# Two pairs of feed-forward units per layer computed with seven block products instead of eight

## The chip, the cores and the metric

The kernel runs on one core of a Trainium2 chip. The metric is the device time of one execution in microseconds (us), from which a median over runs is taken. TensorE does the matrix products, VectorE (DVE) and ScalarE (ACT) the element-wise work, GpSimd (POOL) a few tiny operations, and SyncE's queue (SP) issues the transfers of the weights.

## The reference, cut to what matters

Four layers, each with a feed-forward block, an attention and a second feed-forward block; 256 tokens, width 1024, feed-forward width 2816, all in fp32:

```python
def swiglu(x, w_gate, w_up, w_down):
    return (jax.nn.silu(x @ w_gate) * (x @ w_up)) @ w_down
...
x = x + 0.5 * swiglu(rms_norm(x, norm_g[i, 0]), ffn_w_gate[i, 0], ffn_w_up[i, 0], ffn_w_down[i, 0])
...
x = x + mix @ w_o[i]
x = x + 0.5 * swiglu(rms_norm(x, norm_g[i, 2]), ffn_w_gate[i, 1], ffn_w_up[i, 1], ffn_w_down[i, 1])
```

So there are eight feed-forward blocks. The change touches their gate and up products.

## The kernel before

**Chunks.** All weights are one stream of chunks of 128 x 2048 fp32 (1 MB). Every fp32 product is made of three products of reduced-precision parts: high x high, high x low, low x high. A chunk is loaded by SP into one of three places of `raw`, ScalarE copies it rounded into `w_hi` (`hi`, L376), and VectorE subtracts that from the raw chunk into `w_lo` (`lo`, L629). `w_hi` and `w_lo` are rings of six chunks. SP loads chunk c into a place once the `lo` of chunk c - 3 is done. ScalarE may write a ring slot when TensorE has finished with the chunk six before (`slot_free`).

**Units.** A feed-forward block is cut into eleven units of 256 hidden columns. A unit has three chunks: gate, up (called "top" and "bottom") and down. Units 0 and 1 ("turned") are computed with the tokens on the partitions. Units 2 to 10 ("own") have the hidden columns on the partitions: `own_gate_up` (L1200 to L1205) runs, for each of two banks, eight steps with one matmul of 512 columns (high weights against high and low tokens) and one of 256 (low weights against high tokens). The gate goes to PSUM banks 0 and 1, the up half to banks 2 and 3. Then the down product of the unit before follows: 24 matmuls of 512 columns into `acc` (L1071 to L1073).

**Around a unit.** When the gate half is done, ScalarE copies its second halves out of PSUM (`gate_rest`, L435), VectorE adds (L726), ScalarE applies silu (L438). When the up half is done: ScalarE copies (L440), VectorE adds (L729) and multiplies (L732), ScalarE makes the high part `m_hi` (L443), VectorE the low part `m_lo` (L735). TensorE may start the next unit's gate when L726 is done (`gate_ready`), its up half when L729 is done (`up_ready`), and its down product when L735 is done (`h_split`). In between each engine splits the chunks of the coming units, in an order written out by hand: VectorE's `split_to(c)` means "do all `lo` up to chunk c", ScalarE's the same for `hi`. Every engine works through its own list strictly in order, so what stands behind a waiting instruction waits too. Units 4 to 9 run in a hardware loop of three turns of two units. After the last down product the block's output is added to x and the next input is prepared.

## Time and profile before

| what | value |
|---|---|
| median of 3 runs | 1964.34 us (1964.17 to 1964.35) |
| the profiled execution's own time | 1965.22 us |
| its span in the trace | 1963.4 us |
| granted TensorE clock, mean | 0.996 |
| TensorE / VectorE / ScalarE busy | 99% / 62% / 48% |

The span runs from the first to the last instruction of the trace; the profiled execution took 1.8 us more than its span, and 0.9 us more than the median. "Busy" counts the time in which at least one instruction of the engine runs. A matmul's duration in the trace is longer than the distance to the next one, since they are pipelined: what a stretch costs is read from starts, not from durations.

### The profile page before, as it was taken

The numbers are of one execution on the slowest core, as the hardware profiler recorded it, in microseconds if no ns is written. First come the engines' busy times: TensorE is split into PE (matmuls) and PEld (weight loads), VectorE is DVE, ScalarE is ACT, GpSimd is POOL, SyncE is SP. The second block draws the span as 40 slices with busy tenths as digits, with TensorE's granted clock in tenths as the row PEclk, the third lists the DMA queues.
The fourth block names the chain that finished last, engine by engine and source line by source line (L and its number), as shares of the span: only waits on it lengthen the run. The fifth ranks groups of instructions, "written<-read, shape, count | busy, mean of one in ns | idle before, by whom it ended". The sixth has DMA issues, their size and how long they took to land.

```text
span 1963.4 us, 26311 instructions
## 1 busy us (share of the span) xinstructions
PE 1945.8 (99%) x10556; PEld 1681.9 (86%) x10556; DVE 1219.4 (62%) x1179; ACT 949.7 (48%) x1018; POOL 41.1 (2%) x34
## 2 busy tenths in 40 slices
PE   9999999999999999999999999999999999999998
PEld 7888998888888898888888889988888888988887
DVE  6555657655755678755575555775557556557554
ACT  5444545444544444644454443454445444545443
POOL 0000000000000000100000000000000000000000
PEclk9999999999999999999999999999999999999999
DMA  7654443555455453555445543445554554535541
GB/s 253 234 188 186 157 152 150 206 186 187 186 186 186 168 193 109 185 199 192 172 177 189 191 152 129 171 169 206 186 188 172 193 192 150 194 128 193 191 187 71
DMA packets 49872, 348.80 MB, mean 178 GB/s; under 512 B 6145, under 2 KB 6401, under 8 KB 7937
## 3 DMA queue, kind: packets, MB, share of 16 engines
q1 hardware_dynamic: 49360, 346.54, 47.9%
q8 instruction: 61, 1.00, 0.2%
q10 hardware_dynamic: 432, 1.11, 0.2%
q14 instruction: 19, 0.15, 0.0%
HBM read 346.58 MB, written 1.05 MB: 177 GB/s over the span
## 4 chain that ended last, share of the span: by engine, by line
PE 97%; DVE 2%; DMA 0%; ACT 0%; issue 0%; POOLq 0%; POOL 0%; DVEq 0%; ACTq 0%
PE work L1202 27%; PE work L1200 12%; PE acc L1071 9%; PE acc L1073 9%; PE acc L1072 9%; PE work L1071 7%; PE work L1073 7%; PE work L1072 7%; PE work L1205 2%; PE acc L1115 1%; PE work L1385 1%; DVE w_lo L629 1%; PE work L1372 1%; PE work L1262 0%; DMA x<-x_dram 0%; PE work L1386 0%
## 5 line engine op out<-in xcount | busy, mean ns | idle before, releaser
L629 DVE TENSOR_TENSOR w_lo<-raw,w_hi 128x2048 fp32r<-128x2048 f32 x327 | 746.7, 2288 | 123.7 <-ACT w_hi L376 121.2
L1202 PE MATMUL work<-xn,w_hi 128*128 128x512 f32 x2304 | 795.6, 393 | 0.0
L376 ACT ACTIVATE w_hi<-raw 128x2048 fp32r<-128x2048 f32 x327 | 620.9, 1908 | 16.0 <-DMA raw<-stream_dram 16.0
L1200 PE MATMUL work<-xn,w_lo 128*128 128x256 f32 x2016 | 567.4, 281 | 0.0
L1202 PEld LDWEIGHTS work<-xn,w_hi 128*128 128x128 f32 x2304 | 417.6, 188 | 75.6
L1200 PEld LDWEIGHTS work<-xn,w_lo 128*128 128x128 f32 x2016 | 379.7, 188 | 13.9
L1071 PE MATMUL acc<-w_hi,m_hi 128*128 128x512 f32 x824 | 325.1, 395 | 1.2 <-DVE m_lo L845 0.6
L1073 PE MATMUL acc<-w_hi,m_lo 128*128 128x512 f32 x824 | 321.2, 390 | 0.0
L1072 PE MATMUL acc<-w_lo,m_hi 128*128 128x512 f32 x824 | 320.8, 389 | 0.0
L435 ACT ACTIVATE scratch<-work 128x512 f32<-128x512 f32 x72 | 43.2, 600 | 431.9 <-PE work L1202 431.9
L726 DVE TENSOR_TENSOR scratch<-work,scratch 128x512 f32<-128x512 f32 x72 | 49.8, 692 | 276.3 <-ACT scratch L435 276.3
L1073 PEld LDWEIGHTS acc<-w_hi,m_lo 128*128 128x128 f32 x824 | 154.7, 188 | 32.6
L1071 PEld LDWEIGHTS acc<-w_hi,m_hi 128*128 128x128 f32 x824 | 154.9, 188 | 32.1 <-issue 4.3
L1072 PEld LDWEIGHTS acc<-w_lo,m_hi 128*128 128x128 f32 x824 | 154.9, 188 | 30.8
L1071 PE MATMUL work<-xg,w_hi 128*128 128x256 f32 x512 | 149.7, 292 | 1.2 <-DVE m_lo L827 1.0
L1071 PE MATMUL work<-w_hi,xg 128*128 128x512 f32 x368 | 147.8, 402 | 0.0
L1072 PE MATMUL work<-xg,w_hi 128*128 128x256 f32 x512 | 145.8, 285 | 0.0
L1073 PE MATMUL work<-xg,w_lo 128*128 128x256 f32 x512 | 145.7, 285 | 0.0
L1073 PE MATMUL work<-w_hi,xg 128*128 128x512 f32 x368 | 143.9, 391 | 0.0
L1072 PE MATMUL work<-w_lo,xg 128*128 128x512 f32 x368 | 143.5, 390 | 0.0
L440 ACT ACTIVATE scratch<-work 128x512 f32<-128x512 f32 x72 | 43.1, 598 | 193.2 <-PE work L1202 193.2
L729 DVE TENSOR_TENSOR scratch<-work,scratch 128x512 f32<-128x512 f32 x72 | 49.8, 692 | 110.7 <-ACT scratch L440 110.7
(177 smaller groups left out, 1721.9 us busy)
## 6 DMA issues: line engine op xcount, KB each, us to landing
raw<-stream_dram SPq DMA_DIRECT2D x327, 1024.0 KB, 4.8
x<-x_dram SPq DMA_DIRECT2D x2, 512.0 KB, 7.7
raw<-stream_dram ACTq DMA_DIRECT2D x2, 512.0 KB, 7.4
cst<-consts_dram SPq DMA_DIRECT2D x1, 832.0 KB, 6.8
out_dram<-x SPq DMA_DIRECT2D x3, 256.0 KB, 2.4
final_gain<-final_gain_dram SPq DMA_DIRECT2D x1, 512.0 KB, 7.5
out_dram<-wide SPq DMA_DIRECT2D x1, 256.0 KB, 2.9
cst<-consts_dram ACTq DMA_DIRECT2D x1, 64.0 KB, 1.9
```

What stands on the lines that cost most here:

```text
L376: nc.scalar.activation(w_hi[:, c % RING, :], raw[:, c % RAW, :], ACT.Copy).then_inc(hi_ready, 1)
L435: nc.scalar.activation(gate_rest, own_bank(0)[:, :, T:2 * T], ACT.Copy).then_inc(gate_rest_ready, 1)
L440: nc.scalar.activation(up_rest, own_bank(1)[:, :, T:2 * T], ACT.Copy).then_inc(up_rest_ready, 1)
L629: nc.vector.tensor_tensor(w_lo[:, c % RING, :], raw[:, c % RAW, :], w_hi[:, c % RING, :].bitcast(F32), ALU.subtract).then_inc(lo_ready, 1)
L726: nc.vector.tensor_tensor(gate_sb, own_bank(0)[:, :, 0:T], gate_rest, ALU.add).then_inc(gate_ready, 1)
L729: nc.vector.tensor_tensor(up_sb, own_bank(1)[:, :, 0:T], up_rest, ALU.add).then_inc(up_ready, 1)
L1071: nc.tensor.matmul(dst, a_hi, b_hi, start=start, stop=False, skip_group_check=skip)
L1072: nc.tensor.matmul(dst, a_hi, b_lo, start=False, stop=False, skip_group_check=skip)
L1073: return nc.tensor.matmul(dst, a_lo, b_hi, start=False, stop=stop, skip_group_check=skip)
L1200: nc.tensor.matmul(bank[:, 0:T], lo, xn_hi[:, k, :], start=False, stop=False, skip_group_check=True)
L1202: ins = nc.tensor.matmul(halves(bank), hi, xn[:, :, k, :], start=k == 0, stop=k == DT - 1, skip_group_check=True)
L1205: nc.tensor.matmul(bank[:, 0:T], lo, xn_hi[:, k, :], start=False, stop=False, skip_group_check=True)
```

## The change

In each feed-forward block the units 4 and 5, and the units 8 and 9, are computed together (`SEVEN = 4, 8`). The gate and up columns of two units are 1024 columns; tokens (2 blocks of 128), contraction (2 halves of 512) and columns (2 blocks of 512, one for each unit) form a 2 x 2 by 2 x 2 block product. Instead of eight block products it takes seven, with sums of blocks as operands (Winograd's form). Called by their chunks, in TensorE's order (`PARTS`): b11, t1, t2, b21, t3, t4, b22. Each (`quarter`) is 12 matmuls of 512 columns.

- Four of the seven weight operands are sums of loaded chunks: t1 = b12 - b11, t3 = b22 - b12, t2 = t3 + b11, t4 = b21 - t2. VectorE makes them (`form`) during the unit ahead of the pair (unit 3 or 7), each in a place of its own: t3 over b12, t2 over b11 (both in `raw`), t1 and then t4 in a new place. b22 has a new place too. All seven are then split as other chunks are, so that a pair has seven gate and up chunks to split where two units had four. b11's and b21's places in `raw` come free when t4 is formed.
- Four sums of token blocks (`token_sums`) are formed and split once per block, during unit 2.
- The products come with tokens on the partitions. ScalarE copies two of them out of PSUM (`part_copied`), VectorE makes five sums (`pair_sums_ready`), silu and product are applied in four parts of 256 columns, and TensorE transposes the hidden values of both units (four transposes each) inside the gate half of unit 6 or 10. That unit then carries two down products.
- All hardware loops are gone; the same instructions are written out, SP's too.

The diff, cut to its core (the names of other new functions are in the text above):

```diff
-OWN_UNITS = UNITS - TURNED
-LOOPED = 4
+SEVEN = 4, 8
+PLAIN = [s for s in range(UNITS) if s not in SEVEN and s - 1 not in SEVEN]
+OWN = PLAIN[TURNED:]
+HIDDEN = [s for s in range(UNITS) if s not in OWN]
 PAIRS = D // COLS
-FFN_CHUNKS = 3 * UNITS
+FFN_CHUNKS = 3 * UNITS + 3 * len(SEVEN)
...
+FORMS = "t1", "t3", "t2", "t4"
+PARTS = "b11", "t1", "t2", "b21", "t3", "t4", "b22"
+PAIR_ORDER = *PARTS[:5], "down", *PARTS[5:]
+def ffn_order():
+    order = []
+    for s in range(UNITS):
+        if s in SEVEN:
+            order += [(what, s - (what == "down")) for what in PAIR_ORDER]
+        elif s - 1 in SEVEN:
+            continue
+        elif s - 2 in SEVEN:
+            order += [("top", s), ("down", s - 2), ("bottom", s), ("down", s - 1)]
+        else:
+            order += [("top", s), ("bottom", s)] + [("down", s - 1)] * (s > 0)
+    return order + [("down", UNITS - 1)]
+FFN_ORDER = ffn_order()
...
+            p = no * len(SEVEN) + SEVEN.index(j) if what in PARTS else None
+            if what in ("t1", "t4"):
+                uses.append((what, no, j, SUMS, None))
+            elif what == "b22":
+                uses.append((what, no, j, EXTRA, p + 1))
+            elif what in ("t2", "t3"):
+                uses.append((what, no, j, *places["b11" if what == "t2" else "b12"]))
+            else:
+                uses.append((what, no, j, len(users) % RAW, len(users) // RAW + 1))
+            for load in ("b12",) if what == "t1" else () if what in FORMS or what == "b22" else (what,):
+                r = len(users)
+                places[load] = r % RAW, r // RAW + 1
+                loads.append((load, layer, n % 3, j, r % RAW, users[r - RAW] if r >= RAW else None))
+                users.append(("form", len(FORMS) * (p + 1)) if load in ("b11", "b21") else
+                             ("lo", c0 + order.index(("t3", j)) + 1) if load == "b12" else ("lo", w + 1))
+            if what == "t1":
+                earlier = SEVEN.index(j) - 1
+                loads.append(("b22", layer, n % 3, j, EXTRA,
+                              ("gu", (no * len(PLAIN) + TURNED) * TB) if earlier < 0 else
+                              ("lo", c0 + order.index(("b22", SEVEN[earlier])) + 1)))
...
+                if what in FORMS:
+                    act.wait_ge(form_ready, (no * len(SEVEN) + SEVEN.index(j)) * len(FORMS) + FORMS.index(what) + 1)
+                else:
+                    act.wait_ge(b22_loaded if place == EXTRA else raw_loaded[place], 16 * count)
+                slot_free(act, c)
+                nc.scalar.activation(w_hi[:, c % RING, :], raw_at(place), ACT.Copy).then_inc(hi_ready, 1)
...
+                    after, ahead = s - 2 in SEVEN, s + 1 in SEVEN
+                    if not after:
+                        split_to(g + 3)
+                    if s == TURNED:
+                        hidden_hi(s - 1, unit_bank(s - 1, 0))
+                    if ahead and not after:
+                        split_to(g + 5)
+                    act.wait_ge(top_used, plain + 1)
+                    nc.scalar.activation(gate_rest, own_bank(0)[:, :, T:2 * T], ACT.Copy).then_inc(gate_rest_ready, 1)
+                    split_to(g + (3 if after else 6 if ahead else 4))
+                    act.wait_ge(gate_ready, own_u + 1)
+                    nc.scalar.activation(gate_sb, gate_sb, ACT.Silu).then_inc(own_silu_ready, 1)
+                    if s == TURNED:
+                        token_sums_hi()
+                    if after:
+                        split_to(g + 6)
+                    act.wait_ge(gu_psum, plain * TB + 2)
+                    nc.scalar.activation(up_rest, own_bank(1)[:, :, T:2 * T], ACT.Copy).then_inc(up_rest_ready, 1)
+                    if not after:
+                        split_to(g + (7 if ahead else 5))
+                    act.wait_ge(own_h_ready, own_u + 1)
+                    nc.scalar.activation(m_hi[:, u % 2 * 2:u % 2 * 2 + 2, :], up_sb, ACT.Copy).then_inc(h_hi_ready, 1)
+                    if after:
+                        split_to(g + 7)
...
+                    split_to(q + 5)
+                    copied(1, 0, first_part)
+                    split_to(q + 6)
+                    copied(2, 3, second_part)
+                    split_to(q + 7)
+                    act.wait_ge(part_psum, len(PARTS) * p + 4)
+                    nc.scalar.activation(pair_h[:], work[:, 0, 0:COLS], ACT.Silu).then_inc(pair_silu_ready, 1)
+                    split_to(q + 8)
+                    pair_silu(2, second_sum)
+                    split_to(q + 10)
+                    pair_silu(3, first_part)
+                    pair_silu(4, first_sum)
+                    hidden_hi(s, work[:, 2, :])
+                    hidden_hi(s + 1, work[:, 3, :])
...
+                if what == "t1":
+                    if j == SEVEN[0]:
+                        dve.wait_ge(gu_psum, (no * len(PLAIN) + TURNED) * TB)
+                    dve.wait_ge(raw_loaded[place["t3"]], 16 * USES[q + PAIR_ORDER.index("t3")][4])
+                    ins = nc.vector.tensor_tensor(raw_at(SUMS), b12, b11, ALU.subtract)
+                elif what == "t3":
+                    dve.wait_ge(b22_loaded, 16 * (p + 1))
+                    ins = nc.vector.tensor_tensor(b12, b22, b12, ALU.subtract)
+                elif what == "t2":
+                    dve.wait_ge(form_ready, len(FORMS) * p + 2)
+                    ins = nc.vector.tensor_tensor(b11, b12, b11, ALU.add)
+                else:
+                    dve.wait_ge(form_ready, len(FORMS) * p + 3)
+                    ins = nc.vector.tensor_tensor(raw_at(SUMS), b21, b11, ALU.subtract)
...
+                    if ahead:
+                        form("t1", g + 3)
+                        form("t3", g + 3)
+                        split_to(g + 4)
+                        form("t2", g + 3)
+                        split_to(g + 5)
+                    dve.wait_ge(gate_rest_ready, own_u + 1)
                     nc.vector.tensor_tensor(gate_sb, own_bank(0)[:, :, 0:T], gate_rest, ALU.add).then_inc(gate_ready, 1)
-                    split_next(1)
-                    dve.wait_ge(up_rest_ready, own_u + 1 + turn * 2)
+                    split_to(g + (6 if after or ahead else 4))
+                    if ahead:
+                        form("t4", g + 3)
+                    dve.wait_ge(up_rest_ready, own_u + 1)
                     nc.vector.tensor_tensor(up_sb, own_bank(1)[:, :, 0:T], up_rest, ALU.add).then_inc(up_ready, 1)
-                    dve.wait_ge(own_silu_ready, own_u + 1 + turn * 2)
-                    dve.wait_ge(up_ready, own_u + 1 + turn * 2)
+                    dve.wait_ge(own_silu_ready, own_u + 1)
+                    dve.wait_ge(up_ready, own_u + 1)
                     nc.vector.tensor_tensor(up_sb, up_sb, gate_sb, ALU.mult).then_inc(own_h_ready, 1)
-                    split_next(2)
-                    dve.wait_ge(h_hi_ready, u + 1 + turn * 2)
+                    if not after and not ahead:
+                        split_to(g + 5)
+                    dve.wait_ge(h_hi_ready, u + 1)
                     nc.vector.tensor_tensor(m_lo[:, u % 2 * 2:u % 2 * 2 + 2, :], up_sb,
                                             m_hi[:, u % 2 * 2:u % 2 * 2 + 2, :].bitcast(F32),
                                             ALU.subtract).then_inc(h_split, 1)
-                for turns, body in ffn_steps(step, c0):
-                    with dve.Fori(0, turns) as turn:
-                        body(turn)
-                    split[0] = c0 + 3 * (UNITS - 2) - 1 + RING
+                    if s == TURNED:
+                        token_sums_lo()
+                    if s < UNITS - 1 and (after or ahead):
+                        split_to(g + 7)
...
+                    split_to(q + 5)
+                    dve.wait_ge(part_copied, 2 * p + 1)
+                    part(3)
+                    summed(first_sum, work[:, 1, :], first_part)
+                    split_to(q + 7)
+                    dve.wait_ge(pair_silu_ready, 4 * p + 1)
+                    nc.vector.tensor_tensor(pair_h[:], work[:, 0, COLS:2 * COLS], pair_h[:], ALU.mult).then_inc(pair_h_ready, 1)
+                    part(5)
+                    summed(second_sum, work[:, 1, :], first_part)
+                    dve.wait_ge(part_copied, 2 * p + 2)
+                    dve.wait_ge(pair_sums_ready, 5 * p + 2)
+                    summed(second_sum, second_sum, second_part)
+                    split_to(q + 8)
+                    hidden_of(2, second_sum)
+                    split_to(q + 10)
+                    part(6)
+                    summed(first_part, work[:, 1, :], first_part)
+                    hidden_of(3, first_part)
+                    part(7)
+                    summed(first_sum, work[:, 3, :], first_sum)
+                    hidden_of(4, first_sum)
+                    hidden_lo(s, work[:, 2, :])
+                    hidden_lo(s + 1, work[:, 3, :])
...
+                    pe.wait_ge(gate_ready, own_u + 1)
+                    quarter(0, block_of(0, 0), q, True, False)
+                    pe.wait_ge(up_ready, own_u + 1)
+                    if s == SEVEN[0]:
+                        pe.wait_ge(token_lo_ready, BANKS * (f + 1))
+                    quarter(3, sum_of(S1), q + 1, True, False)
+                    quarter(1, sum_of(S2), q + 2, True, False)
+                    pe.wait_ge(part_copied, 2 * p + 1)
+                    quarter(0, block_of(0, 1), q + 3, False, True)
+                    pe.wait_ge(pair_sums_ready, 5 * p + 1)
+                    quarter(1, sum_of(S3), q + 4, False, False)
+                    unit_down(s - 1).then_inc(down_used, 1)
+                    pe.wait_ge(pair_sums_ready, 5 * p + 2)
+                    quarter(1, block_of(1, 1), q + 6, False, True)
+                    pe.wait_ge(part_copied, 2 * p + 2)
+                    quarter(3, sum_of(S4), q + 7, False, True)
...
+                        if after and at in ((0, DT - 1), (1, DT - 2)):
+                            pair_hidden(p, at[0])
+                    c = c0 + FFN_ORDER.index(("bottom", s))
+                    if after:
+                        unit_down(s - 2).then_inc(down_used, 1)
```

`quarter(bank, part, c, first, last)` waits for `lo` of chunk c and issues the 12 matmuls; `product` is the same three matmuls as before. `token_sums` has four VectorE subtractions or additions of 128 x 512, `token_sums_hi` four ScalarE copies, `token_sums_lo` four VectorE subtractions of that size.

## Rows read from the trace of the kernel before

**Rows 1.** The page, part 1: busy time, share, instructions.
```profile
PE 1945.8 (99%) x10556; PEld 1681.9 (86%) x10556; DVE 1219.4 (62%) x1179; ACT 949.7 (48%) x1018; POOL 41.1 (2%) x34
```

**Rows 2.** The page, part 4: the chain that ended last, by engine.
```profile
PE 97%; DVE 2%; DMA 0%; ACT 0%; issue 0%; POOLq 0%; POOL 0%; DVEq 0%; ACTq 0%
```

**Rows 3.** Windows: stretch, its length, busy per engine, clock, DMA share, GB/s.
```profile
339.42:356.48 17.06, 17.06 (x93) 14.72 (x92) 12.51 (x10) 8.24 (x8) 0.00 (x0) 1.00 0.59 220
356.48:373.10 16.62, 16.62 (x90) 14.31 (x88) 9.47 (x8) 7.64 (x7) 0.00 (x0) 1.00 0.50 190
373.10:389.72 16.62, 16.62 (x90) 14.32 (x89) 9.47 (x9) 7.64 (x7) 0.00 (x0) 1.00 0.51 190
```

**Rows 4.** Timeline of TensorE, first block: start, length, line, shape, count.
```profile
37.86 0.39 PE L1071 MATMUL acc<-w_hi,m_hi 128*128 128x512 f32 x1
...
43.30 0.40 PE L1202 MATMUL work<-xn,w_hi 128*128 128x512 f32 x1
...
54.92 0.39 PE L1071 MATMUL acc<-w_hi,m_hi 128*128 128x512 f32 x1
```

**Rows 5.** Groups by line and shape: count, busy us, mean ns, idle before.
```profile
L629 DVE TENSOR_TENSOR w_lo<-raw,w_hi 128x2048 fp32r<-128x2048 f32 x327 | 746.7, 2288 | 123.7 <-ACT w_hi L376 121.2 <-POOL r_col L351 1.3 <-POOL r_apart L355 1.2
...
L376 ACT ACTIVATE w_hi<-raw 128x2048 fp32r<-128x2048 f32 x327 | 620.9, 1908 | 16.0 <-DMA raw<-stream_dram 16.0
...
L732 DVE TENSOR_TENSOR scratch<-scratch 128x512 f32<-128x512 f32 x72 | 49.9, 693 | 7.5
...
L435 ACT ACTIVATE scratch<-work 128x512 f32<-128x512 f32 x72 | 43.2, 600 | 431.9 <-PE work L1202 431.9
...
L878 DVE TENSOR_TENSOR scratch<-work,cst 128x768 f32<-128x768 f32 x8 | 7.7, 958 | 25.1 <-PE work L1360 25.1
```

**Rows 6.** Timeline of VectorE, second block, units 1 to 3.
```profile
331.87 2.50 DVE L681 TENSOR_TENSOR wide<-wide,r_row 128x512 f32<-128x512 f32 x4
...
339.69 4.48 DVE L629 TENSOR_TENSOR w_lo<-raw,w_hi 128x2048 fp32r<-128x2048 f32 x2
...
355.89 0.69 DVE L735 TENSOR_TENSOR m_lo<-scratch,m_hi 128x512 fp32r<-128x512 f32 x1
356.49 2.29 DVE L629 TENSOR_TENSOR w_lo<-raw,w_hi 128x2048 fp32r<-128x2048 f32 x1
362.90 0.69 DVE L726 TENSOR_TENSOR scratch<-work,scratch 128x512 f32<-128x512 f32 x1 [4.13 <-ACT scratch L435]
```

**Rows 7.** Timeline of VectorE: two splits, each freeing a place of raw.
```profile
691.80 2.29 DVE L629 TENSOR_TENSOR w_lo<-raw,w_hi 128x2048 fp32r<-128x2048 f32 x1
...
697.73 2.28 DVE L629 TENSOR_TENSOR w_lo<-raw,w_hi 128x2048 fp32r<-128x2048 f32 x1
```

**Rows 8.** Timeline of ScalarE: the splits that waited for the loads into those places.
```profile
699.12 1.92 ACT L376 ACTIVATE w_hi<-raw 128x2048 fp32r<-128x2048 f32 x1 [2.10 <-DMA raw<-stream_dram]
704.94 1.92 ACT L376 ACTIVATE w_hi<-raw 128x2048 fp32r<-128x2048 f32 x1 [3.90 <-DMA raw<-stream_dram]
```

**Rows 9.** The page, part 6: transfers, KB each, median us to landing.
```profile
raw<-stream_dram SPq DMA_DIRECT2D x327, 1024.0 KB, 4.8
```

**Rows 10.** Timeline of VectorE, end of the first block.
```profile
192.68 0.69 DVE L735 TENSOR_TENSOR m_lo<-scratch,m_hi 128x512 fp32r<-128x512 f32 x1
```

**Rows 11.** Timeline of TensorE, the first block's last down product.
```profile
193.04 0.39 PE L1073 MATMUL acc<-w_hi,m_lo 128*128 128x512 f32 x1
193.51 0.47 PE L1071 MATMUL acc<-w_hi,m_hi 128*128 128x512 f32 x1
```

**Rows 12.** Windows in the attention of the second layer, columns as in the third group.
```profile
785.00:788.00 3.00, 1.83 (x11) 1.25 (x10) 2.10 (x5) 2.03 (x4) 0.00 (x0) 1.00 0.91 330
788.00:792.00 4.00, 4.00 (x15) 3.23 (x15) 2.21 (x2) 3.00 (x2) 1.06 (x2) 0.58 0.03 10
```

**Rows 13.** Timeline of TensorE in that attention.
```profile
789.72 0.63 PE L1071 MATMUL work<-w_hi,m_hi 128*128 128x512 f32 x1
790.15 0.63 PE L1072 MATMUL work<-w_lo,m_hi 128*128 128x512 f32 x1
```

431 lines of the change are left out of this document (258 added, 173 removed).

## The prediction

> **What bounds the kernel now.** I read the page's first part first: TensorE is busy 99% of the span, VectorE 62%, ScalarE 48% [rows 1]. A share can mislead, so the chain that ended last is next: 97% of it is TensorE's [rows 2]. So a matmul saved is time saved as long as its operands are there in time, and the question is what the spare time of VectorE looks like inside a unit. The windows show a unit as 16.62 us on TensorE, of which VectorE works 9.47 us; it is the same for unit 3, outside the hardware loop, and unit 4, inside it [rows 3]. So writing the loops out neither gains nor costs. VectorE's slack is there in one piece: 4.13 us before L726, right behind the last split it may do [rows 6].
>
> **What is removed.** Starts on TensorE give its prices. From 37.86 to 43.30 us there are 24 matmuls of 512 columns: 0.227 us each. From 43.30 to 54.92 us unit 2 runs its 32 steps of a 512- and a 256-column matmul, with four transposes between [rows 4]. These cost 17.06 - 16.62 = 0.44 us [rows 3], so a step is (11.62 - 0.44) / 32 = 0.349 us. Gate and up of two units: 64 x 0.349 = 22.4 us. Seven products: 84 x 0.227 = 19.0 us. Eight transposes come back in: 2 x 0.44 = 0.9 us. Net per pair -2.44 us, per block -4.9 us, in 8 blocks -39 us. That is the most the change can give.
>
> **What is added on VectorE.** Per pair three more `lo` and four `form`. Back to back a `lo` occupies VectorE for 4.48 - 2.29 = 2.19 us; operations of 512 elements for 0.60 us, since four take 2.50 [rows 6]. The trace has no `form`, a VectorE operation of 2048 elements with fp32 output. From below: 512 elements in fp32 take 693 ns, 768 take 958 [rows 5], so 1.035 ns per element and 0.958 + 1280 x 1.035 = 2.28 us for 2048. From above: the `lo` of that size, 2.288 us [rows 5]. I take the `lo`'s, 2.19 us back to back; with 0.05 us less each the total would be 3 us less. The Trainium skill's page "VectorE: DVE Perf Modes", section "The perf-mode tier table", says that an fp32 `tensor_tensor` has no faster mode, with 2293 ns for 2048 elements: by it the form costs what I take. A copy-like doubled rate, 1.2 us, would all but cancel the loss below; this rule speaks against it. So 7 x 2.19 = 15.3 us more of VectorE per pair, where a unit leaves it 16.62 - 9.47 = 7.2. The pair's unit ahead has to carry most of it; whether it hurts is a matter of order, so I lay it out step by step.
>
> **First pair (second block's clock).** VectorE ends unit 2's `m_lo` at 356.49 us, where before the next split followed at once [rows 6]. TensorE starts unit 3 at 356.48 and would want the pair at 373.10 [rows 3]. VectorE's list is now: four low parts of the token sums, 2.4 (to 358.9); `lo` b11 (361.1); forms t1 and t3 (365.5); `lo` t1 (367.7); form t2, whose result is there at 369.97. ScalarE's `hi` of t2 can only start then, 1.91 [rows 5], to 371.9, with VectorE waiting 2.1 behind it; `lo` t2 (374.2); then gate's add L726, to 374.9. The first product needs gate's banks, so TensorE waits 1.8 us at 373.10. Behind: `lo` b21, form t4 (379.2), up's add L729 (379.9). The first product is over at 377.6 and the second (t1) needs up's banks: wait 2.3 us. In one sentence: VectorE has 23.4 us of work between `m_lo` and up's add, where TensorE takes 16.62 + 2.72.
> The second, the four additions for the token sums themselves in unit 2, 4 x 0.6, lies in the wait before L726 and before the up half's end; L726 moves from 346.3 to 347.4, which nobody wants before 356.48. Cost nothing; without that cover it would push the chain by 2.4.
>
> **Inside the pair.** down3's load takes b11's place in `raw`, which form t4 frees at 379.3. From the end of a `lo` (694.09, 700.01) to the start of the `hi` of the chunk loaded into its place is 5.03 and 4.93 us [rows 7, 8], issue and landing (4.8 [rows 9]) together. So ScalarE starts `hi` of down3 at 384.2, and behind it in its list stands the copy of the first product out of bank 0: 386.0 to 386.6. The fourth product (b21) adds into bank 0 and would start at 379.9 + 2 x 2.72 = 385.3: wait 1.3 us. From there TensorE is not stopped: the sum before t3 is done at 389.0 (wanted 389.4), the down3 split at 388.4 (392.1), b22's at 393.4 (400.3), the sum before top6 at 402.7 (403.0), the transposes' parts at 403.7 and 405.4 (405.8, 408.7), both units' hidden parts at 407.8 and 410.7 (409.5, 414.9). The narrowest is 0.3 us.
>
> **Second pair.** Unit 6 takes two down products and ends at 425.9. down6's load waits for down5's `lo` (414.6), so its `hi` is over at 421.4 and up's copy comes after it; `m_lo` ends at 426.5, `lo` b11 runs 427.6 to 429.8. Then the same list without token sums: forms t1 and t3 (434.2), `lo` t1 (436.4), form t2 (438.7), `hi` and `lo` of t2 (442.9), add (443.6). TensorE wants it at 442.5: waits 1.1, then 2.3 and 1.3 as before.
>
> **Last unit.** ScalarE's `hi` of the next phase's second chunk now stands before up's copy and waits for a load that down9's `lo` frees: it ends at 490.1, while up is over at 489.4. The chain copy, `lo`, add, multiply, high, low ends 0.7 us after TensorE wants the last down product. In the kernel before that place lost 0.2 already: `m_lo` ends 193.37, the matmul starts 193.51 where its pace gives 193.27 [rows 10, 11]. Net 0.5.
>
> **Sum.** Per block: -4.9, +(1.8 + 2.3 + 1.3), +(1.1 + 2.3 + 1.3), +0.5 = +5.7 us. Eight blocks: +46 us. The attention phases and the block ends keep their order and their distance in chunks. Against the span, 1963.4 + 46 = 2009; the execution's own time is 1.8 above its span and 0.9 above the median of the runs, so the median becomes 1964.3 + 46 = 2010 us, slower by 2.3%.
>
> **The rivals.**
> - *Loads land later* (0.08). In the pair, two loads are issued half a microsecond apart, and the last chunks of the block come close together. With 0.7 us more per load that ends a wait, the b21 waits grow by 0.7 each, and so do the second pair's start and the block's end: +2.8 per block, +22 us: 2032. For it: ScalarE waited for loads in the attention [rows 8]. Against: such waits were still only 5 us from `lo` to `hi`.
> - *TensorE's clock falls* (0.09). After a stretch with 1.83 us of matmuls in 3 the granted clock was 0.58 for the next 4 us [rows 12], and 512-column matmuls started 0.43 apart instead of 0.227 [rows 13]; over 4 us that costs 4 x (1 - 0.227 / 0.43) = 1.9 us. That is the 1.2 GHz level. The pair's waits of 1.8 and 2.3 us with 2.7 us of work between are of that kind. But a fall there makes the second and third product slower in front of a wait that only the load ends, and 1.3 of the 1.9 us is absorbed. 0.6 per pair: +10 us: 2020. If nothing absorbs it, 16 x 1.9 = 30: 2040. The Trainium skill's page "TensorE: Matmul & The Clock Gate", section "HAM oscillation", has this as what short work between long waits does on each round; by it, without the absorption, the sum would be the 2040.
> - *Forms at the doubled rate* (0.06), the other side. The bound is where four forms of x us free the chain: at 1.2 us the first waits of both pairs are gone and the second ones 1.0 and 0.3, so that the block comes out 0.3 us below before. At 1.1: 0.9 below, -7 us: 1957. Against: VectorE's rows show one rate for every two-operand form and size [rows 5].
> - *The forms run in slack* (0.04). If the forms could be done in the 4.13 us hole of the unit before [rows 6], nothing is late and the full -39 us stay: 1925. It decides at 2.44 us of wait per pair. Against: the list puts them behind unit 2's `m_lo`, and `raw` has no place for b12 before bottom3 is split.
> - A draw from opposed errors of these (0.03).
>
> **How the numbers follow.** The forecast has 0.70; its own range is 2003 to 2018 (forms 0.05 shorter, -3; a hand-over between engines 0.1 us off at seven waits per block, 6). 0.2% of the time, 4 us, is about what a measurement of this kernel can tell from no change. Slower: 0.70 + 0.08 + 0.09 = 0.87. Faster: 0.10. Same: 0.03. The range takes the forecast and both slower rivals at their likelier price: 1998 to 2033; below it lie the two faster rivals and the draw, 0.13, above it the unabsorbed clock.
>
> **What the profile will show.** TensorE idle before the first product of each pair on L726, before the second on L729, before the fourth on a ScalarE copy; `form` at 2.29 us; VectorE at some 1219 + 16 x 15.3 + 8 x 8 x 0.6 = 1500 us, ScalarE at 950 + 16 x 3 x 1.8 + 8 x 4 x 0.5 = 1050; a pair with its down product 24.5 us plus some 5 us of waits; unit 6 22.9 us. I would be wrong if VectorE's forms are shorter, if the engines' lists run in another order than I read from the diff, or if the clock falls in front of work that nothing covers.

## The result, and the profile of the changed kernel

The changed kernel takes 2016.30 us, the median of 4 runs (2011.96 to 2016.61); the kernel before, on the same chip, 1964.34 (1964.17 to 1965.32). The ratio is 1.0258, with a 95% interval of 1.0241 to 1.0276: slower by 2.6%. The prediction said 2010 with a range of 1998 to 2033. The profiled execution is the shortest of the four, 2011.96 us with a span of 2010.2; the prediction's sum against the span was 2009. The other three lie at 2016.3 to 2016.6, 4.3 us higher, at a mean granted clock of 0.989 to 0.990 where the profiled one has 0.996. So there are two things to explain: the 46.8 us of span, which the trace can show place by place, and the 4.3 us by which the median lies above the profiled execution.

The page of the changed kernel, parts 1, 4 and 6, stands against [rows 1, 2, 9]:

```profile
PE 1925.9 (96%) x9980; PEld 1630.4 (81%) x9980; DVE 1509.1 (75%) x1403; ACT 1047.2 (52%) x1098; POOL 41.1 (2%) x34
```

```profile
PE 59%; DVE 23%; ACT 8%; DMA 7%; issue 2%; POOL 0%; POOLq 0%; DVEq 0%; ACTq 0%
```

```profile
raw<-stream_dram SPq DMA_DIRECT2D x311, 1024.0 KB, 4.9
extra<-stream_dram SPq DMA_DIRECT2D x16, 1024.0 KB, 8.2
```

TensorE's busy time fell by only 19.9 us, not by 39, because a matmul that runs at a lower clock, or that is the last ahead of a wait or the first behind one, is booked longer: in the last experiment below, which has hardly a wait left, the same 9980 matmuls are booked with 1911.6 us. The telling line is the chain: before, 97% of it was TensorE's; now it leaves TensorE for VectorE, ScalarE and a load in four tenths of its length. VectorE is at 75% of the span, far from full, and yet it sets the end. The share over the whole span hides a stretch in which its list takes 23 us, 21 of them work, for 19 us of time.

TensorE's waits, by the line they waited for (total us, times, longest), for weight loads, which count a stall from the first thing that is late:

```profile
PEld work L1285 <- DVE scratch L897: 38.0, 16, 2.4
PEld work L1285 <- DVE scratch L892: 26.6, 16, 2.1
PEld work L1285 <- ACT scratch L544: 17.4, 13, 1.5
```

L892 is gate's add (L726 before), L897 up's add (L729), L544 the copy of the first product out of bank 0. These are the three waits of the prediction, in 16, 16 and 13 of the 16 pairs, and they were not there before. Together 82.0 us, 10.3 per block, where the prediction had 1.8 + 2.3 + 1.3 + 1.1 + 2.3 + 1.3 = 10.1.

What makes them, on VectorE, second block, in the unit ahead of the first pair. Start, length, line, out and in; in brackets the idle time before and who ended it:

```profile
362.24 0.68 DVE L904 TENSOR_TENSOR m_lo<-scratch,m_hi 128x512 fp32r<-128x512 f32 x1
...
365.25 2.28 DVE L753 TENSOR_TENSOR w_lo<-raw,w_hi 128x2048 fp32r<-128x2048 f32 x1
367.45 2.28 DVE L766 TENSOR_TENSOR extra<-raw 128x2048 f32<-128x2048 f32 x1
369.65 2.28 DVE L769 TENSOR_TENSOR raw<-extra,raw 128x2048 f32<-128x2048 f32 x1
371.85 2.28 DVE L753 TENSOR_TENSOR w_lo<-extra,w_hi 128x2048 fp32r<-128x2048 f32 x1
374.06 2.28 DVE L772 TENSOR_TENSOR raw<-raw 128x2048 f32<-128x2048 f32 x1
378.32 2.29 DVE L753 TENSOR_TENSOR w_lo<-raw,w_hi 128x2048 fp32r<-128x2048 f32 x1 [1.99 <-ACT w_hi L459]
380.53 0.68 DVE L892 TENSOR_TENSOR scratch<-work,scratch 128x512 f32<-128x512 f32 x1
381.13 2.28 DVE L753 TENSOR_TENSOR w_lo<-raw,w_hi 128x2048 fp32r<-128x2048 f32 x1
383.33 2.29 DVE L775 TENSOR_TENSOR extra<-raw 128x2048 f32<-128x2048 f32 x1
385.53 0.68 DVE L897 TENSOR_TENSOR scratch<-work,scratch 128x512 f32<-128x512 f32 x1
```

Gate's add is ready when its banks are, long before 380.53, but stands in the list behind four low parts of the token sums (L851, in the stretch left out above), three splits of chunks and three forms. The 1.99 us of idle time in the middle is not slack: VectorE has form t2 ready at 376.3, hands it to ScalarE for the high part, and has nothing that it may do meanwhile. Before, this stretch held 4.13 us of free time right in front of that add [rows 6]. On ScalarE, the same pair:

```profile
390.35 1.92 ACT L459 ACTIVATE w_hi<-raw 128x2048 fp32r<-128x2048 f32 x1 [2.67 <-DMA raw<-stream_dram]
392.18 0.58 ACT L544 ACTIVATE scratch<-work 128x512 f32<-128x512 f32 x1
```

The first of these is down3's high part, waiting for a load into the place that form t4 gave up at 385.6; the copy that TensorE needs stands behind it, although its data were complete at 384, one product of 2.8 us behind 381.27 (below). On TensorE, the three starts of the first pair:

```profile
381.27 0.50 PE L1285 MATMUL work<-w_hi,xn 128*128 128x512 f32 x1 [1.67 <-DVE scratch L892]
...
386.27 0.50 PE L1285 MATMUL work<-w_hi,scratch_r 128*128 128x512 f32 x1 [1.94 <-DVE scratch L897]
...
392.80 0.50 PE L1285 MATMUL work<-w_hi,xn 128*128 128x512 f32 x1 [0.80 <-ACT scratch L544]
```

Unit 3 starts 6.35 us later here than before, because the first block lost that much, so the prediction's times are to be shifted by 6.35: the products were expected at 381.3, 386.2 and 393.0.

The 46.8 us are not made in the feed-forward blocks alone. From the down product in unit 2 to the last matmul into `acc` of the block, the eight blocks together take 48.2 us more than before. The attention of the third layer takes 1.5 us less, 156.8 us against 158.3 up to the down product of the next unit 2, although nothing in it was changed; seven of the eight other traces of this case have 158.3 to 158.5 there, and that with the two short forms 160.0. So the profiled execution was 1.5 us short in a place that the change does not touch.

### The profile page after: what moved, and what is told of

Its sections match the earlier page's. It is cut to its first block, busy times and chain, and to the rows that moved or that the text cites. A ratio compares the mean times of both kernels' runs of the same rounds, so it can differ in the third digit from the quotient of the medians.

```text
span 2010.2 us, 23745 instructions
## 1 busy us (share of the span) xinstructions
PE 1925.9 (96%) x9980; PEld 1630.4 (81%) x9980; DVE 1509.1 (75%) x1403; ACT 1047.2 (52%) x1098; POOL 41.1 (2%) x34
## 4 chain that ended last, share of the span: by engine, by line
PE 59%; DVE 23%; ACT 8%; DMA 7%; issue 2%; POOL 0%; POOLq 0%; DVEq 0%; ACTq 0%
DVE w_lo L753 12%; PE work L1285 11%; PE work L1287 10%; PE work L1286 10%; DMA raw<-stream_dram 7%; PE work L1416 6%; ACT w_hi L459 6%; PE acc L1285 4%; PE acc L1287 4%; PE acc L1286 4%; PE work L1414 3%; DVE raw L772 2%; DVE extra L775 2%; DVE raw L769 2%; DVE extra L766 2%
## 5 line engine op out<-in xcount | busy, mean ns | idle before, releaser
L1416 PE MATMUL work<-xn,w_hi 128*128 128x512 f32 x1280 | 449.4, 394 | 0.0
L1414 PE MATMUL work<-xn,w_lo 128*128 128x256 f32 x1120 | 316.9, 283 | 0.0
L1416 PEld LDWEIGHTS work<-xn,w_hi 128*128 128x128 f32 x1280 | 234.3, 188 | 41.8 <-issue 0.2
L1414 PEld LDWEIGHTS work<-xn,w_lo 128*128 128x128 f32 x1120 | 211.0, 188 | 7.6
L459 ACT ACTIVATE w_hi<-extra 128x2048 fp32r<-128x2048 f32 x48 | 92.0, 1916 | 96.1 <-DVE extra L766 96.1
L1285 PE MATMUL work<-w_hi,xn 128*128 128x512 f32 x192 | 78.9, 411 | 31.8 <-DVE scratch L892 19.9
L753 DVE TENSOR_TENSOR w_lo<-extra,w_hi 128x2048 fp32r<-128x2048 f32 x48 | 108.3, 2283 | 0.0
L1287 PE MATMUL work<-w_hi,wide_r 128*128 128x512 f32 x256 | 101.8, 398 | 0.0
```

Of the source, the lines that this page charges most:

```text
L459: nc.scalar.activation(w_hi[:, c % RING, :], raw_at(place), ACT.Copy).then_inc(hi_ready, 1)
L753: nc.vector.tensor_tensor(w_lo[:, c % RING, :], raw_at(place), w_hi[:, c % RING, :].bitcast(F32), ALU.subtract).then_inc(lo_ready, 1)
L1285: nc.tensor.matmul(dst, a_hi, b_hi, start=start, stop=False, skip_group_check=skip)
L1287: return nc.tensor.matmul(dst, a_lo, b_hi, start=False, stop=stop, skip_group_check=skip)
L1414: nc.tensor.matmul(bank[:, 0:T], lo, xn_hi[:, k, :], start=False, stop=False, skip_group_check=True)
L1416: ins = nc.tensor.matmul(halves(bank), hi, xn[:, :, k, :], start=k == 0, stop=k == DT - 1, skip_group_check=True)
```

## The experiments

The theories. **A**, the prediction's: the loss is made of hand-overs that come late through the order of VectorE's and ScalarE's lists, to which the clock's falls add something. **B**, the rival: one shared cause, VectorE's added work or the pairs' loads, makes everything late, so that an order mended in one place gives far more, or far less, than its timetable says. The kernel before was at 1964.78 us (13 runs) beside the first four and at 1964.87 (7 runs) beside the last four runs of the list.

**The same kernel again.** No edit.

> The changed kernel once more, as a measure for the others. Four executions of it took 2012.0 us once (granted clock 0.996) and 2016.3 to 2016.6 three times (0.989 to 0.990). Theory A (the clock falls in some of the pairs' waits in some executions, and most of it is not absorbed): times at two levels, the longer ones with the lower clock, 4.3 us apart; a profile of an execution with 0.989 shows windows below full clock in feed-forward blocks. Rival B (the clock has no part in the change): its lower clock lies in places that the kernel before has too, and the waits of the pairs show full clock in every trace.

Measured: 2016.20 us (2012.19 to 2016.63), ratio 1.0253 (1.0236 to 1.0270). The runs and their granted clocks are 2012.19 at 0.994, 2015.99 at 0.992, 2016.42 at 0.990, 2016.63 at 0.988: the time goes with the clock. This profile, with a span of 2014.8, is 4.6 us longer than the first. The same windows of both, the first pair of all; columns are stretch, length, busy time and count of TensorE, its weight loads, VectorE, ScalarE, GpSimd, then granted clock, DMA share, GB/s. First the changed kernel's first profile, then this one:

```profile
84.00:88.00 4.00, 4.00 (x18) 3.29 (x19) 3.30 (x3) 0.63 (x1) 0.00 (x0) 1.00 0.79 262
```

```profile
84.00:88.00 4.00, 4.00 (x12) 3.17 (x13) 3.30 (x3) 0.70 (x2) 0.00 (x0) 0.65 0.71 262
```

In the second profile the clock is at 0.65 in a window in which it was full, and 12 matmuls run where 18 did. What it costs can be read from the starts. First the first matmuls of the fourth and the fifth product in the changed kernel's first profile, then two matmuls of the second product and the same two first matmuls in this one:

```profile
90.53 0.50 PE L1285 MATMUL work<-w_hi,xn 128*128 128x512 f32 x1 [0.83 <-ACT scratch L544]
...
93.43 0.39 PE L1285 MATMUL work<-w_hi,wide_r 128*128 128x512 f32 x1
```

```profile
85.50 0.63 PE L1285 MATMUL work<-w_hi,scratch_r 128*128 128x512 f32 x1
85.93 0.63 PE L1286 MATMUL work<-w_lo,scratch_r 128*128 128x512 f32 x1
...
91.06 0.39 PE L1285 MATMUL work<-w_hi,xn 128*128 128x512 f32 x1
...
93.85 0.39 PE L1285 MATMUL work<-w_hi,wide_r 128*128 128x512 f32 x1
```

The matmuls are 0.43 apart, the pace of [rows 13], and the fourth product starts 0.53 us later than in the other profile, with no wait in front of it. The wait for ScalarE has taken up the rest of the fall. By the fifth product the difference is 0.42 us, since a product that starts without a wait is itself 0.11 shorter. Cut into 4-us windows, the first profile has such a fall in 3 of 16 pairs, this one in 10. The waits on L544 bear it out: 13 pairs have one in the first profile, 6 in this one, and they are just the pairs without a fall. From the first to the fifth product a pair takes 14.4 to 14.8 us without a fall and 15.0 with one.

The seven more falls in pairs are not the whole 4.6 us. The eight blocks are 2.9 us longer in this profile, 0.4 us for each of the seven. Another 1.7 us lie in the attention of the third layer, where the clock is low for longer than in the first profile. First that one, then this:

```profile
1220.00:1224.00 4.00, 4.00 (x28) 4.00 (x27) 2.96 (x5) 1.12 (x4) 0.00 (x0) 0.73 0.24 33
```

```profile
1220.00:1224.00 4.00, 4.00 (x17) 3.82 (x18) 0.34 (x2) 0.00 (x0) 0.00 (x0) 0.50 0.01 4
```

In the windows beside these it is 0.85 ahead and 1.00 behind in the first profile, 0.80 ahead and 0.85 behind in this one. The kernel before has the longer kind too, 0.50 and 0.65 in the windows from 1188 to 1196. So theory A's clock term is there, with the absorption, at 0.4 to 0.5 us per fall where the prediction had 0.6; and B's lower clock in places that the kernel before has too is over a third of the difference between the two profiles. The other executions have no trace, so how their 4 us divide is not shown.

**The first product's copy ahead of down3's high part.**

```
                 ...
-                    split_to(q + 5)
                     copied(1, 0, first_part)
                     split_to(q + 6)
```

> ScalarE copies the first product out of its bank before it takes up down3's split, not behind it. Theory A (the third wait is the end of one chain: form t4, load of down3, its two splits, the sum for the fifth product; the copy is only its first customer): the wait before the fourth product goes, one of 1.0 us before the fifth comes, because VectorE's sum stands behind the same split; 0.4 us less per block, so 3 us below the changed kernel. Rival B (the copy's place in ScalarE's list is the cost): 1.0 to 1.3 us per pair, 16 to 21 us less.

Measured: 2010.35 us (2008.94 to 2011.06), ratio 1.0229 (1.0212 to 1.0246). Against the unchanged kernel's median that is -5.9 us, against its two profiles' spans -1.5 and -6.1. The wait on the copy is gone, and most of it stands one step later; the waits on the two adds stay at 38.0 and 26.3:

```profile
PEld work L1284 <- DVE scratch L918: 9.8, 10, 1.2
```

L918 is the sum over the copied product, which VectorE can do only behind down3's low part, and that behind the same load. The line totals, 17.4 and 9.8 us, can't be compared as they are, since the clock fell in 3 pairs there and in 6 here, and such a pair shows no wait of this kind: it is 1.3 us in each of 13 pairs against 1.0 in each of 10, the 1.0 that A expected. Here the wait on a load did not leave with the instruction behind it; it moved to the next one that needs an engine which waits for that load. The drop is somewhat larger than the -3 expected and well short of the 16 to 21 us that B asked for.

**Both adds ahead of the forms.** In the unit ahead of a pair, gate's and up's copies and adds come before the splits of t2 and b21 and before form t4; form t2 stands between the two adds. The cut shows VectorE's list; ScalarE's is changed to match.

```
                     if ahead:
                         form("t1", g + 3)
                         form("t3", g + 3)
                         split_to(g + 4)
-                        form("t2", g + 3)
-                        split_to(g + 5)
                     dve.wait_ge(gate_rest_ready, own_u + 1)
                     ...
-                    split_to(g + (6 if after or ahead else 4))
                     if ahead:
-                        form("t4", g + 3)
+                        form("t2", g + 3)
+                    else:
+                        split_to(g + (6 if after else 4))
                     ...
+                    if ahead:
+                        split_to(g + 6)
+                        form("t4", g + 3)
```

> In the unit ahead of a pair, VectorE makes the gate and up additions (and ScalarE its copies for them) before the second half of the forms and splits; form t4 keeps its place behind b21's split. Theory A (form t4 and the load that it releases set the time): the waits before the first and second product go, the one before the fourth grows from 1.0 to 5.4 and 4.7 us, and the time stays that of the changed kernel, 2012 to 2016; a wait of 5 us may also bring the clock down, which would add up to 1.9 us per pair, 30 us. Rival B (the additions' place in the list is the cost, each wait by itself): 7.5 us less per block, 60 us: 1952 to 1956.

Measured: 2046.53 us (2046.12 to 2048.55), ratio 1.0417 (1.0400 to 1.0435). The short waits are gone, and one long one has come:

```profile
PEld work L1285 <- ACT scratch L542: 81.6, 16, 5.6
```

81.6 us against the changed kernel's 82.0: the same amount, before the fourth product, because the chain form t4, load, down3's high part, copy is now later by what the first two waits were. And yet the span is 2044.6, 34 us longer. The clock, in the second block, and the matmul that opens the fourth product:

```profile
396.00:400.00 4.00, 3.78 (x9) 3.04 (x10) 4.00 (x3) 4.00 (x4) 0.00 (x0) 0.50 0.84 287
```

```profile
396.22 0.80 PE L1285 MATMUL work<-w_hi,xn 128*128 128x512 f32 x1 [5.21 <-ACT scratch L542]
```

Behind this wait of 5.2 us the clock is at 0.50, the 1.2 GHz level of the two, and the matmul takes 0.80 us instead of 0.50. Such a fall is there in all 16 pairs, behind waits of 4.2 to 5.2 us on TensorE, and behind it there is no further wait into which the lost time could go: 34 / 16 = 2.1 us per pair, beside the prediction's 1.9. Of the 34 us 33.3 lie in the eight blocks; single pairs lose from 1.3 to 2.8. The Trainium skill's page "TensorE: Matmul & The Clock Gate", section "HAM oscillation", has falls as what work between long waits brings on each round; by that rule all 16 pairs lose the time, and here the trace agrees, while in the changed kernel only 3 and 10 of 16 did.

**Form t4 right behind form t2.** Form t4 waits for b21's load itself, and the places of b11 and b21 in `raw` come free with the low part of t2 and of b21 instead of with form t4.

```
-                users.append(("form", len(FORMS) * (p + 1)) if load in ("b11", "b21") else
+                users.append(("lo", c0 + order.index(("t2", j)) + 1) if load == "b11" else
                 ...
                         form("t2", g + 3)
+                        form("t4", g + 3)
                         split_to(g + 5)
                     ...
                     split_to(g + (6 if after or ahead else 4))
-                    if ahead:
-                        form("t4", g + 3)
```

> VectorE makes form t4 right behind form t2, where it waited 2 us for ScalarE's split of t2; everything else keeps its order (down3's load now waits for t2's low part, down4's for b21's). Theory A (the hole behind form t2 and the late release of down3's load are the cost): up's addition comes 2.2 us earlier in VectorE's list, the second and third waits go, the first stays at 2.1 and 1.3 us; per block 6.6 us less than the changed kernel, 52 us: 1960 to 1964, the level of the kernel before. Rival B (VectorE has too much work there, whatever its order): the same sum of work, no more than the 2 us hole per pair, 2012 to 2016 less up to 32 us.

Measured: 1968.71 us (1962.62 to 1971.75, 10 runs), ratio 1.0013 (1.0003 to 1.0022), 47.5 us less than the unchanged kernel. The one long wait left is the one on gate's add:

```profile
PEld work L1285 <- DVE scratch L894: 30.6, 16, 2.3
```

Of the other two 1.7 us are left in all, on up's add in 10 pairs, as both had form t4 in their chain: the hole of 1.99 us holds it now, where VectorE waited for ScalarE. The median is above the 1960 to 1964 expected, and the reason is the clock, which fell in 6 of the 16 pairs of the profiled execution. The first block's first pair has no fall. Its first and fourth product:

```profile
77.99 0.50 PE L1285 MATMUL work<-w_hi,xn 128*128 128x512 f32 x1 [1.92 <-DVE scratch L894]
...
86.36 0.39 PE L1285 MATMUL work<-w_hi,xn 128*128 128x512 f32 x1
```

The second block's first pair has one:

```profile
372.00:376.00 4.00, 2.21 (x5) 1.82 (x6) 4.00 (x4) 3.08 (x4) 0.00 (x0) 0.73 0.41 131
```

```profile
373.79 0.79 PE L1285 MATMUL work<-w_hi,xn 128*128 128x512 f32 x1 [1.92 <-DVE scratch L894]
...
383.71 0.39 PE L1285 MATMUL work<-w_hi,xn 128*128 128x512 f32 x1
```

The two products are 8.37 us apart without a fall and 9.92 with one: 1.5 us, in each of the six. The waits that absorbed a fall were themselves taken away, so it costs some three times what it did in the changed kernel. Without the six falls (6 x 1.53 = 9.2) the span would be some 1968.7 - 9.2 = 1959.5, and the time some 1961 (an estimate from these rows). That the runs spread over 9 us for the same reason is likely but not shown: the longest, 1971.75, had a granted clock of 0.991, but the shortest, 1962.62, had 0.994, and two at 0.995 and 0.996 took 1965.

**Two forms made short.** The prediction's bound on the forms, tried by leaving work out: t3 and t2 take in 128 of their 2048 columns.

```
-                    ins = nc.vector.tensor_tensor(b12, b22, b12, ALU.subtract)
+                    dve.wait_ge(form_ready, len(FORMS) * p + 1)
+                    ins = nc.vector.tensor_tensor(b12[:, 0:P], b22[:, 0:P], b12[:, 0:P], ALU.subtract)
                 ...
-                    ins = nc.vector.tensor_tensor(b11, b12, b11, ALU.add)
+                    ins = nc.vector.tensor_tensor(b11[:, 0:P], b12[:, 0:P], b11[:, 0:P], ALU.add)
```

> Leaves out most of two weight sums: forms t3 and t2 work on 128 of their 2048 columns (so the products t3, t2 and t4 have other operands); everything else stays. Theory A (the waits are VectorE's list being too long): two forms become 0.2 instead of 2.2 us; the first wait goes, the second stays at 2.0 and 1.3, the third at 1.0; 4.2 us less per block, 33 us: 1979 to 1984. Rival B (what holds TensorE is the crossing to ScalarE and back behind form t2 and the loads, not the forms' length): no more than 1 us per pair, 1996 and more.

Measured: 1977.77 us (1975.19 to 1978.48), ratio 1.0062 (1.0045 to 1.0079), just below the 1979 to 1984 expected by A. The wait on gate's add is gone:

```profile
PEld work L1286 <- DVE scratch L898: 28.0, 16, 2.2
PEld work L1286 <- ACT scratch L544: 20.9, 16, 1.4
```

The two that are left make up 48.9 us. Some 4 us of VectorE's 15.3 per pair are taken away and (2016.2 - 1977.8) / 16 = 2.4 us per pair of time come back, where moving form t4 alone, with all the work kept, brought 3.0. So the amount of VectorE's work in that stretch counts, but it is not what the time goes by alone. No pair of this trace has a fall of the clock.

**The up copy ahead of a split in units 6 and 10.**

```
                     if after:
-                        split_to(g + 6)
+                        split_to(g + 5)
                     act.wait_ge(gu_psum, plain * TB + 2)
                     nc.scalar.activation(up_rest, own_bank(1)[:, :, T:2 * T], ACT.Copy).then_inc(up_rest_ready, 1)
+                    if after:
+                        split_to(g + 6)
```

VectorE's list is changed in the same way: its split to g + 6 stands behind the product of gate and up.

> In units 6 and 10 ScalarE copies the up half, and VectorE adds and multiplies it, before they take up the chunk whose load is late (down6, and the next phase's second chunk). Theory A (second pair's first wait and the wait at the block's end come from these two loads): the first wait of the second pair (1.1) goes, its second shrinks to 1.7, the last down product's to 0.2; 2.1 us less per block, 17 us: 1995 to 2000. Rival B (the second pair is late by its own forms, as the first): the wait at the block's end alone, 0.5 per block, 4 us: 2008 to 2012.

Measured: 1998.93 us (1997.17 to 2000.59), ratio 1.0173 (1.0156 to 1.0190). Waits on gate's add are left in the 8 first pairs only:

```profile
PEld work L1289 <- DVE scratch L894: 16.7, 8, 2.1
```

So the 1.1 us before each second pair came from unit 6, whose up copy stood behind a high part that waited for a load, and not from the pair's own forms.

**The token sums' low parts ahead of unit 2's up add.**

```
+                    if s == TURNED:
+                        token_sums_lo()
                     dve.wait_ge(up_rest_ready, own_u + 1)
                     ...
-                    if s == TURNED:
-                        token_sums_lo()
```

> The four low parts of the token sums are made before unit 2's up addition, where VectorE waits 1.5 us for ScalarE's copy, and not behind it. Theory A (2.4 us of them stand at the head of the list that makes the first pair late): the first pair's first wait goes and its second is 2.0, the second pair is as before; 2.1 us less per block, 16 us: 1996 to 2000. Rival B (they are hidden in unit 3 as it is): 2012 to 2016.

Measured: 1998.88 us (1998.07 to 1999.98), ratio 1.0174 (1.0157 to 1.0190). The 2.4 us that stood behind `m_lo` at the head of unit 3's list now lie in unit 2, where VectorE has time. The wait on gate's add is gone from the first pairs, but for 0.5 us in one, and stays at 1.1 to 1.3 in the second pairs:

```profile
PEld work L1285 <- DVE scratch L892: 9.8, 9, 1.3
```

**The three edits together.** Form t4 early, the up copy early, the token sums early.

> Three of these edits together: form t4 right behind t2, the up copy ahead of the late loads in units 6 and 10, the low parts of the token sums ahead of unit 2's up addition. Theory A (the orders of work are the whole loss, and seven products are worth 2.44 us per pair): no wait over 0.2 us at the pairs, no fall of the clock there; 4.6 us less per block than the kernel before: 1964 - 37 = 1927. Rival B (VectorE's sum of work, 75% busy, does not allow it; waits turn up elsewhere): 1940 to 1960.

Measured: 1933.02 us (1932.50 to 1933.89), ratio 0.9839 (0.9823 to 0.9856): faster than both kernels, 1.6% below the one before. That is 6 us above the 1927 that A expected. Part 1 of its page, its chain, and the longest wait at a pair that is left (the next, on up's add, is 1.4 us in all):

```profile
PE 1911.6 (99%) x9980; PEld 1630.8 (84%) x9980; DVE 1507.0 (78%) x1403; ACT 1049.6 (54%) x1098; POOL 41.0 (2%) x34
```

```profile
PE 95%; DVE 3%; issue 1%; ACT 0%; DMA 0%; POOL 0%; POOLq 0%; DVEq 0%; ACTq 0%
```

```profile
PEld work L1289 <- DVE scratch L896: 3.2, 8, 0.7
```

VectorE does as much as in the changed kernel, 1507.0 against 1509.1 us, and the same 9980 matmuls run. The span is 32.4 us below the kernel before, 4.1 per block where the matmuls were to save 4.9. 0.4 of that is the wait on L896 in the first pairs. The other 0.4 is in the products themselves. Starts of the fourth, the fifth and the next down product in the second block, on TensorE:

```profile
377.11 0.39 PE L1289 MATMUL work<-w_hi,xn 128*128 128x512 f32 x1
...
379.90 0.39 PE L1289 MATMUL work<-w_hi,wide_r 128*128 128x512 f32 x1
...
382.63 0.39 PE L1289 MATMUL acc<-w_hi,m_hi 128*128 128x512 f32 x1
```

A product whose stationary operand, the one that the weight load brings in, is `xn` takes 2.79 us, the others 2.73 and the down products 2.72. Three of the seven read `xn`: 3 x 0.07 = 0.2 us per pair, 3.3 us in all. So the saving is 39 - 3.3 = 35.7, and 1963.4 - 35.7 + 3.2 is the span, 1931.0, to 0.1 us. That leaves nothing for the loops that were written out. No pair has a fall of the clock. B, which asked for 1940 to 1960 because VectorE's added work stays, is out. The list of VectorE in the unit ahead of the first pair, second block:

```profile
361.27 2.29 DVE L774 TENSOR_TENSOR raw<-raw 128x2048 f32<-128x2048 f32 x1
363.59 2.29 DVE L778 TENSOR_TENSOR extra<-raw 128x2048 f32<-128x2048 f32 x1
365.80 2.29 DVE L755 TENSOR_TENSOR w_lo<-raw,w_hi 128x2048 fp32r<-128x2048 f32 x1
```

Form t4 (L778) fills the hole between form t2 (L774) and t2's low part, and nothing waits there.

## Why the prediction was right, step by step

- **The saving, 39 us.** The first term of the sum, and 3.3 us too large: the version with all three edits bears out 35.7, since the price of 0.227 us per matmul came from down products, and those that read `xn` start 0.232 apart.
- **The forms.** Costed at 2.28 to 2.288 us, 2.19 back to back; the group by line of form t1 shows the first, the starts 367.45, 369.65 and 371.85 shown further up the second (2.20 apart). The doubled rate is out.

```profile
L766 DVE TENSOR_TENSOR extra<-raw 128x2048 f32<-128x2048 f32 x16 | 36.6, 2285 | 0.0
```

- **VectorE and ScalarE in total.** Forecast 1500 and 1050; measured 1509.1 and 1047.2.
- **The first and the second wait of the first pair.** Forecast 1.8 and 2.3; gate's add was to end at 381.2 (374.9 + 6.35) and ends at 381.21, the products start at 381.27 and 386.27 where 381.3 and 386.2 stood. The experiment with form t4 moved shows that the second hangs on form t4, those with the token sums and the short forms that the first hangs on the length of the list ahead of it.
- **The 23.4 us of work.** The number is right as a time (362.84 to 386.21 us, 23.4) but not as work: 2.0 us of it is the hole behind form t2, as the prediction's own steps have it. That matters for the cure, since form t4 fits into that hole. In the version with all three edits the same list, without the token sums' low parts, runs from 352.46 to 371.49, 19.0 us for 19.3.
- **The third wait.** Forecast 1.3, found 1.0: the fourth product starts at 392.80 instead of 393.0, since down3's high part starts at 390.35, 4.7 us after the end of form t4 and not 4.9 to 5.0. The step holds, its size was 0.2 to 0.3 too large. It is there in 13 pairs, with falls of the clock in 3; in the second profile of the same kernel in 6, with falls in 10.
- **The second pair.** Forecast 1.1, 2.3 and 1.3, by down6's load holding back unit 6's up copy. Its products start at 450.02, 455.02 and 461.73; the timetable had 449.96, 454.9 and 461.7. The edit that lets the copy go first removed exactly the first of them.
- **The last unit, 0.5.** The last down product starts 0.41 us late behind `m_lo`:

```profile
501.10 0.39 PE L1287 MATMUL acc<-w_hi,m_lo 128*128 128x512 f32 x1
501.90 0.47 PE L1285 MATMUL acc<-w_hi,m_hi 128*128 128x512 f32 x1 [0.41 <-DVE m_lo L904]
```

  From 501.10 at its pace it would start at 501.33; it loses 0.57, before it lost 0.24 [rows 11]. So the net is 0.3 there, not 0.5.
- **Per block.** Unit 2 starts at 345.77 and the last down product 156.13 us later, where before it was 150.21: +5.9, forecast +5.7. The saving was 0.4 too large. With 4.5 saved, the waits and the last unit cost 10.4, where the forecast had 10.6, 0.2 too long. These errors have opposite signs and partly cancel, so the sum is a little better than its terms. Three falls of the clock add some 1.3 us, and with them the eight blocks come to about the 48.2 measured, where 46 were forecast.
- **The rivals.** Later loads: out, no load that ends a wait is later than forecast. The doubled rate and the slack: out. The clock: this is where the prediction's form was at fault. It set the fall of the clock as a case that replaces the forecast, 2020 or 2040, where it is an amount that varies from one execution to the next: 3 pairs in one, 10 in another. The likeliest sum had no term for it. That it met the profiled span to 1 us is in part luck: it was 2.2 us short in the blocks, and that execution was 1.5 us short in the third attention. In the second profile, 4.6 us longer, 2.9 are falls in pairs that the sum lacks and 1.7 are that attention. The price of a fall was sized a little high where a wait absorbs most of it (0.6, measured 0.4 to 0.5), and lies between the two measured where nothing does (1.9; 1.5 with form t4 early, 2.1 behind the long waits).

## What to carry to other kernels

Where an engine's share leaves room but work is added in one place, write down its list between two deadlines of the engine that bounds the kernel: a list that takes 23 us for 19 us of time loses 4 us, whatever the share over the span is. Mark its holes as well as its work: 2 us of the 23 were idle. Look in that list for the instruction that others wait for and for what stands ahead of it without need, above all something that itself waits for a load; here the same matmuls and the same added work cost 52 us or gave back 32 by their order alone. Count what a late hand-over does to the clock of TensorE as a term, and don't take away the wait that hides it without the one that causes it.

## What the runs showed of the hardware that was not expected

- The two loads of a pair that are issued 0.4 us apart (356.76 and 357.13 in the second block): the one into `extra` takes 8.2 us at the median from issue to landing, the loads into `raw` 4.9. No engine waited for it in the changed kernel; in a chain that ends with it, it would be some 3.4 us more than the 4.8 used in the prediction.
- Falls of the clock are not the same from one execution to the next at waits of the same length: with waits of 1.1 to 2.4 us 3, 10 and 6 pairs of 16 had one (the changed kernel twice, the one with form t4 early), 6 with the first product's copy early, 4 with the up copy early, 8 with the token sums early, none with the short forms; with all three edits, where no wait at a pair is over 0.7 us, none had one; behind waits of 4.2 to 5.2 us all 16 had one. What decides it in a single pair stays open.
- A fall costs what is left of it after the next wait: 0.4 to 0.5 us where one follows, 1.5 where none does (form t4 early), 2.1 behind the long waits.
- The clock also falls in the attention of the third layer in every trace here, and there it is low for longer in some executions than in others: 1.7 us between two profiles of one kernel. A difference of that size between two single profiles is not the change's.
- Matmuls of one size are not all paced alike: 0.227 us apart with `m_hi` or the sums as the stationary operand, 0.232 with `xn`. Why was not tried.
